# Moving the load of a modulation tile by three places in the weight queue of a hybrid decoder trunk

## The reference

```python
sh1, sc1, g1, sh2, sc2, g2, sh3, sc3, g3 = ada_modulation(c, w['w_ada'], w['b_ada'])   # silu(c) @ w + b, 9 parts of 1024
h = modulate(rms_norm(x, w['norm_ffn1']), sh1, sc1)
x = x + 0.5 * g1 * swiglu(h, w['w_ffn1_in'], w['w_ffn1_out'])      # 1024 -> 2 x 2816 -> 1024
h = modulate(rms_norm(x, w['norm_mix']), sh2, sc2)
u = h @ w['w_in']                                                  # four mixers: SSD, RG-LRU, HGRN2, MLA
...
x = x + g2 * (y @ w['w_out'])
h = modulate(rms_norm(x, w['norm_ffn2']), sh3, sc3)
x = x + 0.5 * g3 * swiglu(h, w['w_ffn2_in'], w['w_ffn2_out'])
```

## Time and the profile before

| | |
|---|---|
| three runs | 1968.76, 1974.93 and 1982.86 us, median 1974.93 |
| profiled execution | 1967.89 us, span 1966.2 us, mean granted TensorE clock 0.926 |
| busy | PE 1773.0 us, PEld 1482.2, DVE 904.7, ACT 611.5, POOL 187.7 |
| moved | 272.06 MB, mean 138 GB/s |

### The profile page before, as it was taken

One profiled execution on the slowest core, in us unless ns is written; L12 is line 12 of the kernel. 1 busy time (PEld: TensorE's weight loads), 2 busy tenths in 40 slices (PEclk: granted clock), 3 DMA queues, 4 the chain that ended last, 5 costly groups with the idle time before them and its releaser, 6 DMA issues.

```text
span 1966.2 us, 28925 instructions
## 1 busy us (share of the span) xinstructions
PE 1773.0 (90%) x12084; PEld 1482.2 (75%) x12084; DVE 904.7 (46%) x1642; ACT 611.5 (31%) x831; POOL 187.7 (10%) x336
## 2 busy tenths in 40 slices
PE   4799989999768988999989998989987689899998
PEld 3799987776534567999979998967755355599998
DVE  2443343475576224434453332436756642444443
ACT  2433331033321324333343332311423133243331
POOL 0000002610034000000000000063002220000000
PEclk8899999999777889999989999999987689999999
DMA  9466455432011562655546555463310128335442
GB/s 312 143 214 195 145 179 156 147 96 67 3 50 37 176 215 66 214 193 182 161 129 193 193 193 167 149 183 92 103 33 22 43 71 270 115 99 159 144 157 69
DMA packets 260314, 272.06 MB, mean 138 GB/s; under 512 B 10860, under 2 KB 255058, under 8 KB 260184
## 3 DMA queue, kind: packets, MB, share of 16 engines
q1 hardware_dynamic: 247308, 250.50, 40.0%
q0 software_dynamic: 12000, 19.63, 3.9%
q10 hardware_dynamic: 876, 0.09, 0.0%
HBM read 264.68 MB, written 5.50 MB: 137 GB/s over the span
## 4 chain that ended last, share of the span: by engine, by line
PE 80%; DVE 12%; ACT 3%; DMA 2%; SPq 1%; issue 1%; DVEq 0%; ACTq 0%
PE bank L805 15%; PE bank L807 15%; PE bank L806 15%; PE bank L906 9%; PE bank L1342 4%; PE bank L734 3%; PE bank L1031 3%; PE bank L1213 2%; PE bank L752 1%; PE bank L765 1%; DMA ring<-in_w_ada_dram 1%; DVE big L1912 1%; DMA ring<-in_w_ffn_out_dram 1%; DVE big L1992 1%; PE bank L1256 1%
## 5 line engine op out<-in xcount | busy, mean ns | idle before, releaser
L807 PE MATMUL bank<-hT_r,ring_r 128*128 128x320 f32 x1408 | 437.9, 311 | 0.0
L807 PEld LDWEIGHTS bank<-hT_r,ring_r 128*128 128x128 f32 x1408 | 267.8, 190 | 0.0
L805 PE MATMUL bank<-hT_r,lat_pages_r 128*128 128x320 f32 x704 | 220.6, 313 | 14.0 <-DVE gates_r L1683 13.9
L1666 DVE TENSOR_TENSOR ring_r<-ring,lat_pages_r 128x2048 fp32r<-128x2048 f32 (+1 forms) x68 | 151.3, 2229 | 172.1 <-ACT lat_pages_r L1373 172.1
L807 PE MATMUL bank<-big_r,ring_r 128*128 128x320 f32 x704 | 218.8, 311 | 0.0
L806 PE MATMUL bank<-gates_r,lat_pages_r 128*128 128x320 f32 x704 | 218.8, 311 | 0.0
L906 PE MATMUL bank<-hT,ring 128*128 128x320 f32 x736 | 208.7, 443 | 7.5 <-DVE hT L1679 7.5
L906 PEld LDWEIGHTS bank<-hT,ring 128*128 128x128 f32 x736 | 142.4, 195 | 66.4 <-issue 11.2
L1373 ACT ACTIVATE lat_pages_r<-ring 128x2048 fp32r<-128x2048 f32 (+1 forms) x68 | 126.5, 1861 | 150.9 <-DMA ring<-in_w_ffn_out_dram 66.7
L805 PEld LDWEIGHTS bank<-hT_r,lat_pages_r 128*128 128x128 f32 x704 | 133.6, 190 | 22.6 <-issue 20.0
L1414 ACT ACTIVATE sq<-bank 128x320 f32<-128x320 f32 x88 | 38.2, 435 | 309.1 <-PE bank L807 309.1
(11 more groups left out here) (521 smaller groups left out, 3132.0 us busy)
## 6 DMA issues: line engine op xcount, KB each, us to landing
ring<-in_w_ffn_in_dram SPq DMA_DIRECT2D x88, 1024.0 KB, 5.4
ring<-in_w_ada_dram SPq DMA_DIRECT2D x40, 1024.0 KB, 6.6
sqk<-in_w_ada_dram SPq DMA_DIRECT2D x32, 1024.0 KB, 7.6
ring<-in_w_ffn_out_dram SPq DMA_DIRECT2D x32, 1024.0 KB, 5.5
ring<-in_w_in_dram SPq DMA_DIRECT2D x20, 1024.0 KB, 5.4
ring<-in_w_ffn_out_dram SPq DMA_DIRECT2D x16, 768.0 KB, 6.0
lat_pages<-in_cache_mla_latent_dram POOLq DMA_DIRECT2D x128, 64.0 KB, 2.1
ring<-in_w_out_dram SPq DMA_DIRECT2D x8, 1024.0 KB, 11.2
```

The lines of the kernel that those rows point to most:

```text
L805: mm(out, w_h, x_h, start=start, stop=False)
L807: return mm(out, w_l, x_h, start=False, stop=stop)
L1666: go(v.tensor_tensor(slot_r(n, nk, 256), slot(n, nk, 256), w_hi_r[(w * FT + i) % HI][:, 0:nk].bitcast(F32), ALU.subtract), w_low)
```

## The change

The load of the twelfth modulation tile (x = 11) stands behind tile 28 of the first network and no more behind tile 25. The other eleven, and all of the other engines' programs, stay as they are. `KF` is 22, and j is the tile's number in the network less 3.

```diff
                             sp.dma_start(slot(n, chunks, width), src).then_inc(slot_loaded[n % RING], 16)
                             j = n - tile_of(l, T_FFN[0]) - 3
-                            if j >= 0 and j % 2 == 0 and j // 2 < 12:
+                            if j >= 0 and j % 2 == 0 and j // 2 < 11:
                                 aux_load(sp, l, j // 2, l, ADA_AHEAD + j // 2)
+                            if j == KF + 3:
+                                aux_load(sp, l, 11, l, ADA_AHEAD + 11)
```

## The result

Five executions of the changed kernel took 1953.03 to 1957.95 us, median 1956.16, beside a median of 1976.63 for five of the kernel before; the ratio is 0.9902, with a 95% interval of 0.9883 to 0.9922. The forecast was 1957 us and 15.2 us less than 1971.8, a ratio of 0.9923; it lies at the upper edge of the first interval, just outside, and within the second. One execution of all those told here, of the kernel with one layer moved, took 5569.99 us; why is not known, and its median and ratio leave it out.

The account below looks back on a forecast made before the run. TensorE was taken as the bound, busy 90% of the span, so a load pays only where TensorE halts. Removing the halts gains 15.2 us, added places and mixers 0: from 1971.8 to 1957 us, range 1946 to 1969.

Parts of the forecast that it names:

- The halt at tile 26: First network's output half, each layer: tile 26 queued behind the modulation load's 21.4 us wait; removing it gains 15.2 us.
- The second way of sizing: First network's output half against the second network's, less 3.1 us extra work: 7.7 and 7.5 us, together 15.2.
- The first way of sizing: Between tiles 25 and 26 and just after: 5.4 us idle plus 1.9 us lower clock, 7.3 us a layer.
- The rule cited from the Trainium skill: Around tile 26: lowered clock time costs half of itself, 3.4 us; with the idle time 8.8 us a layer.
- What stands late next: Output half after tile 26: later weight tiles and the modulation load have 8 to 12 us cover, so cost nothing.
- Wanted only at 274: Tile 28 in the output half: lands near 252, ready near 256, wanted by TensorE only at 274 us.
- The halt didn't move on to tile 29: Rival, chance 0.05: tile 29 comes late instead, the 7.7 us paid three tiles later; 1972 us, no change.
- the modulation tile came in time: Rival, chance 0.02: twelfth modulation tile late, TensorE halts after tile 27; 1975 us at a 30 us landing.
- The dearer low clock: Rival, chance 0.07: low clock around tile 26 costs more than matmuls show; gain 17.6 us, giving 1954.
- The mixers' clock: Both layers' mixers: 0, with 2.2 us a layer either side; slower-clock rival, chance 0.04, 1991 us at 0.83.
- the middle of the known times: Whole kernel: forecast's starting point, (1968.76 + 1974.93) / 2 = 1971.8 us, from all four known times.

Follow-up runs that it names:

- the halt filled and the order changed: Kernel before with 36 useless matmuls ahead of tile 26, and tile 28's high and low part behind the first two squares and residuals: 1983.23 us.
- the halt filled alone: Kernel before with 36 matmuls of no use on TensorE between tiles 25 and 26, load left in place: 1978.72 us, ratio 1.0023.
- the two that kept TensorE busier in the first network: Kernel before with 36 useless matmuls ahead of tile 26, without and with tile 28's parts moved behind squares and residuals: 1978.72 and 1983.23 us.
- the one behind tile 26 with the changed order: Changed kernel with the load behind tile 26, tile 28's high and low part behind the first two squares and residuals: 1956.41 us, ratio 0.9905.

## Why the prediction was right

*The halt at tile 26* was right in place, cause and size. The second way of sizing gave 7.7 and 7.5 us a layer, and the halves shrank by 7.6 and 7.3; they were forecast at about 84 us and took 84.3 and 84.4.

*The first way of sizing*, 7.3 us, was right as well. The halves lost the idle 5.4 and 5.3 us, and TensorE's busy time in them fell by 86.50 - 84.30 = 2.2 and 86.36 - 84.40 = 2.0 us, where 1.9 had been put for the low clock; with the halt filled and the order changed it was 1.8. The two prices add up here because the change takes away both and brings tile 28 early too. They do not add up for every change: with the halt filled alone, the wait for the sums and, in layer 1, for tile 26 itself took back half or all of the second. The rule cited from the Trainium skill, page "TensorE: Matmul & The Clock Gate", section "HAM oscillation — how this bites in real kernels", which prices lowered time at half of itself, gave 3.4 us for all 6.8 us of low clock and was not borne out. Taken over the 4.30 us in which matmuls ran, 4.1 us of low clock by the prediction's own sum, the half would be 2.1, close to the 2.0 to 2.2 measured.

*What stands late next.* The forecast asked when TensorE wants tiles 27, 28 and 29 and the modulation tile, found covers of many microseconds, and none of them was waited for. But for tile 28 it asked the wrong question. "Wanted only at 274" is true of TensorE; DVE and ACT come past it in their own order much earlier, ahead of the squares that TensorE wants near 267. With the load moved by three places tile 28 is early on every engine: in the changed kernel its low part is done at 257.9, the squares at 261.0, and TensorE comes to the sums at 268.7. So the slip cost nothing, which is luck as far as tile 28 goes. With one place it would have cost 4.7 and 4.4 us.

*The rivals.* The halt didn't move on to tile 29, and the modulation tile came in time: the waits above name neither. The dearer low clock, 8.8 us a layer, fell with the halves.

*The mixers' clock* was put at nothing, with 2.2 us a layer on both sides. Between the two profiled executions this held: by the marks of the earlier trace rows the mixers of the changed kernel took 424.3 and 422.3 us, at 0.87 and 0.88. As a bound on what can happen it was too small. Over the profiled executions of all these kernels, the stretch with the mixer of layer 0 took 605.8 to 613.2 us and that of layer 1 592.8 to 601.2, with the same work in it, though the four of the kernel before stayed within a microsecond of one another. A spread of 8 us is as large as what one layer of the change is worth. It may be why two comparisons of the same pair gave 0.990 and 0.993; no long execution of the pair was profiled, so that is not shown.

*The time.* That it came out at 1956 us for a forecast of 1957 is partly luck. The forecast starts from the middle of the known times, 1971.8, which lies between the two groups of executions, and not from the profiled one, which was among the shortest and would have given 1952.7.

## What to carry to other kernels

A load that waits for a consumer should stand in a queue behind all the loads whose places are already free, as far as its own cover allows (behind tile 32 it had none); look for the longest wait of the queue, and count what stands behind it. Then ask of every load that comes late not only when its main consumer wants it but which in-order engine must pass it earlier, since its place there holds up other work. And size a stall also by comparing the stage with a twin that has none, which takes in all that follows from the stall (here 7.7 us, against 7.3 from the two stretches and 7.6 measured).

## What was not expected of the hardware

Executions of one and the same kernel make two groups, with medians of 1969.2 and 1975.0 us and mean granted clocks near 0.926 and 0.923. Where in the kernel the clock differs was not seen for the kernel before. In the edited kernels the stretches with the mixers differ: the two that kept TensorE busier in the first network had them 2 to 8 us longer a layer, at 0.89 and 0.90. The added work can't be all of it, since the kernel with the load behind tile 27 had 600.5 us in layer 1 at 0.89, and the one behind tile 26 with the changed order 611.2 us in layer 0, without any. What shifts the clock stays open.

Also, a tile of 1 MB took longer to land the more loads were issued just ahead of it. Alone, ACT could begin on it some 5.7 us after its issue. Of the tiles issued right behind the modulation load, the first took 7.7 to 7.9 us in most executions (9.06 once), the second 9.4 (behind tile 26) and the third 11.2 and 12.3 (the filled halt, layers 0 and 1).
